# Sums of squares before the norms of a hybrid encoder layer: one f32 matmul each, or two matmuls on rounded squares and rests, and column sums in another PSUM bank

## The chip, the core and the metric

The kernel runs on one core of one Trainium2 chip. The metric is the device time of one execution in microseconds (us), the median of several runs. All times of the profile come from one profiled execution.

## The reference, cut to what matters

One encoder layer on x of 512 tokens by 2048 features, in float32:

```python
h = rms_norm(x, norm_mix_pre) * (1 + sc1) + sh1
proj = h @ w_in                       # q (8 heads), k, v (2 heads each), five groups of 8 recurrent heads
q = rms_norm(q, q_norm_w); k = rms_norm(k, k_norm_w)      # over the 128 features of a head
q = rope(q) * 128 ** -0.5; k = rope(k)
o_att = softmax(q @ k.T) @ v
o_hg = bidirectional_gated_recurrence(...)                # 8 heads, chunkwise in the reference
o_hg = rms_norm(o_hg, out_norm) * silu(gate)              # over the 128 features of a head
x = x + g1 * rms_norm(concat(o_att, o_hg) @ w_out, norm_mix_post)
x = x + g2 * rms_norm(conv_glu_ffn(rms_norm(x, norm_ffn_pre) * (1 + sc2) + sh2), norm_ffn_post)
```

What matters here are the sums over 128 features that the norms of 2 keys, 8 queries and 8 recurrent heads need: 18 in all, each for 512 tokens.

## The kernel before

**Layout.** Activations lie with features on the 128 partitions and the 512 tokens along the row, so that a head is one 128x512 tile. A sum over a head's features is then a sum over partitions. It is made on TensorE: the squares (`SQA` for keys and queries, `SQ` for recurrent heads) stream through a 128x128 matrix of ones, and every partition of a PSUM bank (`PB[2]`, `PB[5]`) gets the sum. A matmul with plain f32 operands is recorded as two weight loads and two matmuls.

**Three passes.** The projections multiply in three passes of rounded numbers (type fp32r): ScalarE writes the rounded copy (`W_hi`, `H_hi`), VectorE the rest (`W_lo`, `H_lo`), and `three_passes` (L2131) adds lo*hi, hi*hi and hi*lo in a bank. Such a matmul is one weight load and one matmul.

**Steps.** From about 147 us to 900 us the work is an order written out by hand. TensorE's outer loop are projection tiles of 16 steps; `project_step` is one step, three passes of 128x512. Between the steps, at step numbers fixed in the code, every engine has its side work: `kv_side` (2 keys and 2 values, beside the first tile), `att_side` (h, s) and `att_tail` (eight attention heads, one tile of 16 steps each), then `hg_side` (p, g) with g from 0 to 79 for a recurrent head p beside the five tiles of the next one. VectorE and ScalarE have the same loops with their own branches for the same step numbers. Each engine works through its list strictly in the order of the code; semaphores join them. The splits of the weights (`split_hi` on ScalarE, `split_lo` on VectorE) stand in the same lists, at steps 4 and 6 (VectorE one step later) of a tile, in recurrent heads at every eighth step.

**A norm of keys or queries** (index r: 0 and 1 are keys, 2 to 9 queries). ScalarE squares the head into `SQA` (`rope_front`, L825), TensorE sums it (`rope_mm`, L2158, at steps 1 and 7 for the keys, step 1 for a query), ScalarE makes Ln and Exp of the sum (`rope_rs`, L845 and L847, with a table load before each), which is the factor `RSA`. VectorE (`rope_back`) meanwhile multiplies the head by cosines and its rotated copy by sines (L1463, L1465), adds (L1467), and multiplies by `RSA` (L1472). Then the query is split into `Q_hi` and `Q_lo` (L887, L1502), and the `scores` matmuls start at step 7. `att_values` (L2198), at step 4, writes the bank that `rope_mm` wrote, and so waits until the Ln of the same tile's query has read it.

**A norm of recurrent heads.** At g = 72 ScalarE squares bank 4 into `SQ` (L1018), at g = 73 TensorE sums it (`sum_squares`, L2346) into bank 5, at g = 74 ScalarE makes Ln and Exp (L1023, L1025), at g = 76 VectorE writes the result (L1624).

**Column sums of the modulation.** Beside each of the eight projection heads VectorE adds up 16 rows of `w_ada` in `AB_acc`; at g = 77 and 78 `sum_chunk` (L2375) sums its columns with two groups of four 128x1 matmuls, also into bank 5, and `chunk_take` (L1643) copies the eight numbers out. Because the bank is shared, `sum_chunk` waits for `o_rstd`, which the Exp of the norm raises, and `turn_hg_values` of the next head (four transposes into bank 5) waits for `chunk_taken`.

Of the kernel before, what the change touches and what calls it, by code (L numbers as in the profile page):

```python
# [154 lines left out]
def hybrid_encoder_layer(nc, x, c, w_ada, b_ada, norm_mix_pre, norm_mix_post, w_in, q_norm, k_norm,  # L155
# [17 lines left out]
    ones = at("ones", [P, P], F32, C0 + 512)  # L173
    VEC = at("VEC", [P, 768], F32, C0 + 1536)
# [44 lines left out]
    SQA = at("SQA", [P, S], F32, OV + 12 * KB)  # L219
    RSA = at("RSA", [P, S], F32, OV + 14 * KB)  # L220
# [17 lines left out]
    SQ = at("SQ", [P, S], F32, OV + 24 * KB)  # L238
    RS = at("RS", [P, S], F32, OV + 26 * KB)
# [59 lines left out]
    with ExitStack() as ctx:  # L299
# [22 lines left out]

        rope_in, rope_psum, rope_rstd, rope_ln, rope_t, rope_done = (
# [427 lines left out]
        def _(act):  # L751
# [35 lines left out]
            act.activation(SM[:, LBT:LBT + 32], SM[:, LBT:LBT + 32], ACT.Exp).then_inc(lb_exp, 1)  # L787
            act.wait_ge(shift_added, KT)
# [33 lines left out]
            def rope_front(r, src):  # L822
                if r:
                    act.wait_ge(rope_psum, r)
                act.activation(SQA[:, :], src, ACT.Square).then_inc(rope_in, 1)  # L825
# [47 lines left out]
            def att_store(h):  # L873
                act.wait_ge(att_pv, h + 1)
                act.activation(MX[:, HEADS[h], :], PB[2][:, :], ACT.Copy).then_inc(att_out, 1)
# [13 lines left out]
            def att_side(h, s):  # L889
                if s == 0:  # L890
                    query_front(h)
                if s == 2:
                    rope_rs(h + KV_HEADS)
# [23 lines left out]
            def key_front(g):  # L917
                act.wait_ge(k_kept, g + 1)
                rope_front(g, KR[:, g, :])
# [65 lines left out]
            def hg_side(p, g):  # L985
# [30 lines left out]
                if g == 72:  # L1016
                    act.wait_ge(av_done, p + 1)
                    act.activation(SQ[:, :], PB[4][:, :], ACT.Square).then_inc(o_squared, 1)  # L1018
# [302 lines left out]
        def _(dve):  # L1321
# [136 lines left out]
            def rope_back(r, src, turned, w, w_turned, dst, gates=()):  # L1458
                if r == 0:
                    dve.wait_ge(tables_landed, 32)  # L1460
                else:
                    dve.wait_ge(rope_done, r)
                dve.scalar_tensor_tensor(T1[:, :], src, w, COS[:, :], ALU.mult, ALU.mult).then_inc(rope_t, 1)  # L1463
# [136 lines left out]
            def hg_side(p, g):  # L1600
# [16 lines left out]
                if g == 73:  # L1617
                    dve.wait_ge(o_squared, p + 1)
                    dve.tensor_tensor(OG[:, :], PB[4][:, :], GW[:, :], ALU.mult).then_inc(o_gated, 1)
# [20 lines left out]
            def chunk_take(h):  # L1640
                dve.wait_ge(chunk_summed, h + 1)
                dst = MOD[:, 32 + 8 * h:40 + 8 * h] if isinstance(h, int) else MOD[:, bass.ds(h * 8 + 32, 8)]
                dve.tensor_copy(dst, PB[5][:, 0:8]).then_inc(chunk_taken, 1)  # L1643
# [410 lines left out]
        def _(pe):  # L2054
# [95 lines left out]
            def rope_mm(r):  # L2150
                pe.wait_ge(rope_in, r + 1)
                if r == 0:
                    pe.wait_ge(front_kept, 1)
# [4 lines left out]
                pe.matmul(PB[2][:, :], ones[:, :], SQA[:, :], start=True, stop=True).then_inc(rope_psum, 1)  # L2158
# [501 lines left out]
```

## Time and profile before

| | before |
|---|---|
| median of 3 runs | 2378.36 us (2376.03 to 2379.28) |
| span of the profiled execution | 2375.8 us |
| PE, matmul | 2334.7 us busy (98%) |
| PEld, weight loads | 2025.8 us (85%) |
| DVE (VectorE) | 1878.8 us (79%) |
| ACT (ScalarE) | 1104.8 us (47%) |
| POOL | 128.6 us (5%) |

The span goes from the first to the last recorded instruction of the profiled execution. The page gives no device time of that execution apart from its span; the span lies 2.6 us below the median of the timed runs and 0.2 us below the fastest of them.

How to read it: the busy time of PE is modelled from pipelined matmuls and overstates how full it is; a 128x512 matmul is recorded with 0.39 us, though the next one starts sooner. The start times of successive weight loads (PEld) show TensorE's pace. In a timeline row "x2" means two instructions in one row, and the bracket at the end is the idle time of the engine just before, with what ended it. An instruction's record on ACT or DVE can overlap the next one's by up to 0.1 us. PEclk is the granted TensorE clock as a share of 2.4 GHz.

### The profile page before, as it was taken

How to read it: one execution, taken by the hardware profiler on the slowest of the kernel's cores; microseconds unless marked ns; L12 is line 12 of the kernel's file. 1: busy time of each engine (PE TensorE's matmuls, PEld its weight loads, DVE VectorE, ACT ScalarE, POOL GpSimd, SP SyncE). 2: the span in 40 equal slices, each digit the busy share in tenths (PEclk: the TensorE clock that was granted, in tenths of full speed). 3: DMA queues.
4: the chain of work that ended last, by engine and by line, in shares of the span. 5: the costliest groups of instructions: out<-in, count | busy, mean ns of one | idle time of the engine just before them, and what ended most of it. 6: DMA issues, size and time to landing. Idle time of an engine off the chain costs nothing.

```text
span 2375.8 us, 37218 instructions
## 1 busy us (share of the span) xinstructions
PE 2334.7 (98%) x13671; PEld 2025.8 (85%) x13671; DVE 1878.8 (79%) x2447; ACT 1104.8 (47%) x1517; POOL 128.6 (5%) x207
## 2 busy tenths in 40 slices
PE   6999999999999999999999999999999999999998
PEld 3577778888888877878999999999999998888887
DVE  5875667887777873267799999999999998888777
ACT  4266744334443353254444444444444445555554
POOL 1010000000000000000000000000000000001100
PEclk9999999999999999999999999999999999999999
DMA  9952456666666734336555555555555559779966
GB/s 366 346 157 85 133 180 208 215 219 212 207 211 198 234 89 169 98 124 159 146 140 146 145 144 143 144 142 139 141 145 145 142 176 329 251 207 285 279 226 224
DMA packets 378834, 442.47 MB, mean 186 GB/s; under 512 B 14876, under 2 KB 295716, under 8 KB 376448
## 3 DMA queue, kind: packets, MB, share of 16 engines
q1 hardware_dynamic: 359056, 369.74, 49.1%
q0 software_dynamic: 19696, 71.68, 13.0%
q8 instruction: 46, 0.75, 0.1%
q14 instruction: 36, 0.29, 0.0%
HBM read 418.81 MB, written 66.08 MB: 204 GB/s over the span
## 4 chain that ended last, share of the span: by engine, by line
PE 87%; DVE 5%; DMA 3%; ACT 2%; issue 2%; SPq 0%; DVEq 0%; ACTq 0%
PE bank L2132 26%; PE bank L2134 26%; PE bank L2133 26%; DMA ADA<-in_w_ada_dram 2%; PE bank L2295 2%; DVE ACC L1373 2%; DMA AB_raw<-in_w_ada_dram 1%; PE bank L2198 1%; DVE ZZ L1577 1%; PE bank L2375 1%; PE bank L2314 1%; PE bank L2189 1%; DVE W_lo L1332 0%; PE bank L2063 0%; DVE AB_acc L1636 0%
## 5 line engine op out<-in xcount | busy, mean ns | idle before, releaser
L2132 PE MATMUL bank<-H_lo,W_hi 128*128 128x256 f32 (+1 forms) x1832 | 635.7, 347 | 0.0
L2134 PE MATMUL bank<-H_hi,W_lo 128*128 128x256 f32 (+1 forms) x1832 | 613.6, 335 | 0.0
L2133 PE MATMUL bank<-H_hi,W_hi 128*128 128x256 f32 (+1 forms) x1832 | 613.2, 335 | 0.0
L2132 PEld LDWEIGHTS bank<-H_lo,W_hi 128*128 128x128 f32 x1832 | 349.3, 191 | 35.8 <-issue 6.2
L2133 PEld LDWEIGHTS bank<-H_hi,W_hi 128*128 128x128 f32 x1832 | 349.3, 191 | 35.7 <-issue 6.2
L2134 PEld LDWEIGHTS bank<-H_hi,W_lo 128*128 128x128 f32 x1832 | 348.8, 190 | 35.6
L2132 PE MATMUL bank<-T_lo,W_hi 128*128 128x256 f32 x1280 | 362.2, 283 | 0.0
L2133 PE MATMUL bank<-MGR,W_hi 128*128 128x256 f32 x1280 | 362.2, 283 | 0.0
L2134 PE MATMUL bank<-MGR,W_lo 128*128 128x256 f32 x1280 | 362.2, 283 | 0.0
L2132 PEld LDWEIGHTS bank<-T_lo,W_hi 128*128 128x128 f32 x1280 | 245.8, 192 | 0.0
L2133 PEld LDWEIGHTS bank<-MGR,W_hi 128*128 128x128 f32 x1280 | 245.8, 192 | 0.0
L2134 PEld LDWEIGHTS bank<-MGR,W_lo 128*128 128x128 f32 x1280 | 245.8, 192 | 0.0
L1332 DVE TENSOR_TENSOR W_lo<-W_raw,W_hi 128x1024 fp32r<-128x1024 f32 x138 | 168.1, 1220 | 94.6 <-ACT W_hi L765 94.2
L2132 PE MATMUL bank<-W_lo,GS_hi 128*128 128x512 f32 x616 | 240.0, 390 | 1.7 <-DVE W_lo L1941 1.7
L2134 PE MATMUL bank<-W_hi,GS_lo 128*128 128x512 f32 x616 | 239.7, 389 | 0.0
L2133 PE MATMUL bank<-W_hi,GS_hi 128*128 128x512 f32 x616 | 239.7, 389 | 0.0
L1168 ACT ACTIVATE W_hi<-UB 128x1024 fp32r<-128x1024 f32 x160 | 164.1, 1049 | 148.6 <-DVE UB L1810 95.1
L1798 DVE TENSOR_TENSOR W_lo<-UB,W_hi 128x1024 fp32r<-128x1024 f32 x160 | 195.1, 1220 | 26.9 <-ACT W_hi L1168 26.9
L765 ACT ACTIVATE W_hi<-W_raw 128x1024 fp32r<-128x1024 f32 x138 | 144.8, 1050 | 77.4 <-PE bank L2134 44.6
L1636 DVE SCALAR_TENSOR_TENSOR AB_acc<-AB_raw,SM,AB_acc 128x1024 f32<-128x1024 f32 x120 | 153.6, 1280 | 16.9 <-DMA AB_raw<-in_w_ada_dram 15.7
L1168 ACT ACTIVATE W_hi<-W_raw 128x1024 fp32r<-128x1024 f32 x80 | 84.5, 1056 | 150.6 <-DVE W_raw L1810 98.3
L2132 PEld LDWEIGHTS bank<-W_lo,GS_hi 128*128 128x128 f32 x616 | 115.6, 188 | 27.0 <-DVE W_lo L1941 2.5
(311 smaller groups left out, 3741.7 us busy)
## 6 DMA issues: line engine op xcount, KB each, us to landing
AB_raw<-in_w_ada_dram SPq DMA_DIRECT2D x128, 512.0 KB, 4.4
UB<-in_w_up_dram SPq DMA_DIRECT2D x100, 512.0 KB, 4.1
W_raw<-in_w_in_dram SPq DMA_DIRECT2D x90, 512.0 KB, 4.8
t_dram<-in_w_down_dram POOLq DMA_DIRECT2D x88, 512.0 KB, 8.1
DRAW<-in_w_down_dram SPq DMA_DIRECT2D x66, 512.0 KB, 5.8
W_raw<-in_w_up_dram SPq DMA_DIRECT2D x56, 512.0 KB, 3.9
ADA<-in_w_ada_dram SPq DMA_DIRECT2D x48, 512.0 KB, 9.0
W_raw<-in_w_down_dram SPq DMA_DIRECT2D x44, 512.0 KB, 6.1
```

The lines of the kernel that those rows point to most:

```text
L765: act.activation(W_hi[:, k % SLOTS, :], W_raw[:, k % RAW, :], ACT.Copy).then_inc(hi_ready, 1)
L1168: act.activation(units(W_hi[:, (U_ST + PRODUCTS * jj + p) % SLOTS, :]), ST[e][ST_UNIT[p]], ACT.Copy)\
L1332: dve.tensor_tensor(W_lo[:, k % SLOTS, :], W_raw[:, k % RAW, :], W_hi[:, k % SLOTS, :].bitcast(F32), ALU.subtract).then_inc(lo_ready, 1)
L1373: ins = dve.scalar_tensor_tensor(ACC[g][:, :], src, col(SM, CS + r), ACC[g][:, :], ALU.mult, ALU.add)
L1577: ins = dve.tensor_tensor(v, v, t[:, :, :, other].unsqueeze(3).broadcast_to([P, 2, n, m]), ALU.mult)
L1636: ins = dve.scalar_tensor_tensor(AB_acc[:, :], AB_raw[:, kt % 2, :], col(SM, CS + kt), AB_acc[:, :], ALU.mult, ALU.add)
L1798: dve.tensor_tensor(units(W_lo[:, slot, :]), ST[e][ST_UNIT[p]], units(W_hi[:, slot, :].bitcast(F32)), ALU.subtract)\
L2132: pe.matmul(acc, st_hi, mv_lo, start=start, stop=False, skip_group_check=on)
L2133: pe.matmul(acc, st_hi, mv_hi, start=False, stop=False, skip_group_check=on)
L2134: return pe.matmul(acc, st_lo, mv_hi, start=False, stop=stop, skip_group_check=on)
L2189: ins = pe.transpose(PB[6 + qt % 2][:, k * P:(k + 1) * P], PM[qt][:, k * P:(k + 1) * P], ident[:, :])
L2295: ins = pe.matmul(bank[:, a * P:(a + 1) * P], KM[:, a * P:(a + 1) * P], queries, start=True, stop=True)
```

## The change

The squares get a rounded copy (`SQA_hi`, `SQ_hi`) and a rest (`SQA_lo`, `SQ_lo`), and the sum is two fp32r matmuls with a rounded matrix of ones, `ones_r`. This goes for 17 of the 18 sums: the last recurrent head keeps its f32 matmul at g = 73. ScalarE squares twice (the second time in f32), VectorE has a new subtraction, and `rope_mm` waits for it (`squares_low`) before its second matmul. `rope_mm` moves from steps 1 and 7 to 2 and 8 for the keys, and from 1 to 2 for queries; `sum_squares` from g = 73 to 75. `SQA_hi` lies in a row of `MX` that holds the input activations before and an attention output after, so two waits are added. The column sums go to bank 6 and no longer wait for `o_rstd`.

```diff
+    ones_r = at("ones_r", [P, P], F32R, C0 + 1024)
+    SQA_lo = at("SQA_lo", [P, S], F32R, OV + 12 * KB)
+    SQA_hi = at("SQA_hi", [P, S], F32R, MXB + HEADS[-2] * 2 * KB)
+    SQ_lo = at("SQ_lo", [P, S], F32R, OV + 24 * KB)
+    SQ_hi = at("SQ_hi", [P, S], F32R, OV + 36 * KB)
...
+            act.wait_ge(consts_landed, 16)
+            act.activation(ones_r[:, :], ones[:, :], ACT.Copy).then_inc(lb_exp, 1)
...
             def rope_front(r, src):
                 if r:
                     act.wait_ge(rope_psum, r)
+                act.activation(SQA_hi[:, :], src, ACT.Square)
                 act.activation(SQA[:, :], src, ACT.Square).then_inc(rope_in, 1)
...
             def att_store(h):
                 act.wait_ge(att_pv, h + 1)
+                if h == ATT_HEADS - 2:
+                    act.wait_ge(rope_psum, ATT_HEADS + KV_HEADS)
...
-                if s == 2:
+                if s == 3:
                     rope_rs(h + KV_HEADS)
...
             def key_front(g):
                 act.wait_ge(k_kept, g + 1)
+                act.wait_ge(h_lo, KT)
...
                 if g == 72:
                     act.wait_ge(av_done, p + 1)
+                    if not (isinstance(p, int) and p == HG_HEADS - 1):
+                        act.activation(SQ_hi[:, :], PB[4][:, :], ACT.Square)
...
                     dve.wait_ge(rope_done, r)
+                dve.wait_ge(rope_in, r + 1)
+                dve.tensor_tensor(SQA_lo[:, :], SQA[:, :], SQA_hi[:, :].bitcast(F32), ALU.subtract).then_inc(squares_low, 1)
                 dve.scalar_tensor_tensor(T1[:, :], src, w, COS[:, :], ALU.mult, ALU.mult).then_inc(rope_t, 1)
...
                 if g == 73:
                     dve.wait_ge(o_squared, p + 1)
+                    if not (isinstance(p, int) and p == HG_HEADS - 1):
+                        dve.tensor_tensor(SQ_lo[:, :], SQ[:, :], SQ_hi[:, :].bitcast(F32), ALU.subtract).then_inc(squares_low, 1)
...
-                dve.tensor_copy(dst, PB[5][:, 0:8]).then_inc(chunk_taken, 1)
+                dve.tensor_copy(dst, PB[6][:, 0:8]).then_inc(chunk_taken, 1)
...
-                pe.matmul(PB[2][:, :], ones[:, :], SQA[:, :], start=True, stop=True).then_inc(rope_psum, 1)
+                pe.wait_ge(rope_in, r + 1)
+                pe.matmul(PB[2][:, :], ones_r[:, :], SQA_hi[:, :], start=True, stop=False)
+                pe.wait_ge(squares_low, r + 1)
+                pe.matmul(PB[2][:, :], ones_r[:, :], SQA_lo[:, :], start=False, stop=True).then_inc(rope_psum, 1)
...
-                if s == 1:
+                if s == 2:
                     rope_mm(h + KV_HEADS)
...
-                if s in (1, 7):
-                    rope_mm(s // 7)
+                if s in (2, 8):
+                    rope_mm(s // 8)
...
                 pe.wait_ge(vt_ready, p + 1)
-                pe.wait_ge(chunk_taken, p + 1)
+                if not (isinstance(p, int) and p == 0):
+                    pe.wait_ge(o_ln, p)
...
-                if g == 73:
+                if g == (73 if isinstance(p, int) and p == HG_HEADS - 1 else 75):
                     sum_squares(p)
...
-                    if not first:
-                        pe.wait_ge(o_rstd, h)
+                    if first:
+                        pe.wait_ge(pt_ready, ATT_HEADS * TT)
+                    else:
+                        pe.wait_ge(chunk_taken, h)
                 for j in range(4 * half, 4 * half + 4):
-                    ins = pe.matmul(PB[5][:, j:j + 1], AB_acc[:, j * P:(j + 1) * P], ones[:, 0:1], start=True, stop=True)
+                    ins = pe.matmul(PB[6][:, j:j + 1], AB_acc[:, j * P:(j + 1) * P], ones[:, 0:1], start=True, stop=True)
```

`sum_squares` has the same pair of matmuls with `SQ_hi` and `SQ_lo` for all heads but the last.

How VectorE's list moves at the keys, in the order of issue. `T` is the rotated sum, `KTT` the finished key, `W_lo` the rest of a weight tile. Before:

```order
L1463 SCALAR_TENSOR_TENSOR T_108<-KR,VEC,COS 128x512 [waits tables_landed,k_kept]
L1465 SCALAR_TENSOR_TENSOR KTT<-KROT,VEC,SIN 128x512 [waits rot_landed0]
L1467 TENSOR_TENSOR T_108<-T_108,KTT 128x512 [waits rope_t]
L1472 TENSOR_TENSOR KTT<-T_108,RSA 128x512 [waits rope_rstd,rope_t]
L1332 TENSOR_TENSOR W_lo<-W_raw,W_hi 128x1024 [waits hi_ready] x2
L1463 SCALAR_TENSOR_TENSOR T_108<-KR,VEC,COS 128x512 [waits rope_done,k_kept]
```

And with the change:

```order
L1478 TENSOR_TENSOR SQA_lo<-SQA,SQA_hi 128x512 [waits rope_in,tables_landed,k_kept]
L1479 SCALAR_TENSOR_TENSOR T_111<-KR,VEC,COS 128x512
L1481 SCALAR_TENSOR_TENSOR KTT<-KROT,VEC,SIN 128x512 [waits rot_landed0]
L1483 TENSOR_TENSOR T_111<-T_111,KTT 128x512 [waits rope_t]
L1488 TENSOR_TENSOR KTT<-T_111,RSA 128x512 [waits rope_rstd,rope_t]
L1346 TENSOR_TENSOR W_lo<-W_raw,W_hi 128x1024 [waits hi_ready] x2
L1478 TENSOR_TENSOR SQA_lo<-SQA,SQA_hi 128x512 [waits rope_in,rope_done,k_kept]
L1479 SCALAR_TENSOR_TENSOR T_111<-KR,VEC,COS 128x512
```

The new subtraction of each key stands at the head of `rope_back`; the second key's stands behind two subtractions for weights.

TensorE's list at the end of a recurrent head, from the sum of squares on. Before, with four steps between the sum of squares and the column sums, of which the first stands here:

```order
L2346 MATMUL bank<-SQ,ones 128x512 [waits o_squared]
L2132 MATMUL bank<-H_lo,W_hi 128x512
L2133 MATMUL bank<-H_hi,W_hi 128x512
L2134 MATMUL bank<-H_hi,W_lo 128x512
...
L2375 MATMUL bank<-ones,AB_acc 128x1 [waits o_rstd,chunk_added]
L2375 MATMUL bank<-ones,AB_acc 128x1 x3
```

And with the change:

```order
L2371 MATMUL bank<-SQ_hi,ones_r 128x512 [waits o_squared]
L2373 MATMUL bank<-SQ_lo,ones_r 128x512 [waits squares_low]
L2150 MATMUL bank<-H_lo,W_hi 128x512
L2151 MATMUL bank<-H_hi,W_hi 128x512
L2152 MATMUL bank<-H_hi,W_lo 128x512
...
L2404 MATMUL bank<-ones,AB_acc 128x1 [waits chunk_taken,chunk_added]
L2404 MATMUL bank<-ones,AB_acc 128x1 x3
```

Two steps now lie between the pair and the column sums, and the column sums wait for the copy of the head before in place of this norm's Exp.

## Rows read from the trace of the kernel before

**Rows 1.** The page: busy time of PE; the chain that ended last, by engine
```profile
PE 2334.7 (98%) x13671; PEld 2025.8 (85%) x13671; DVE 1878.8 (79%) x2447; ACT 1104.8 (47%) x1517; POOL 128.6 (5%) x207
PE 87%; DVE 5%; DMA 3%; ACT 2%; issue 2%; SPq 0%; DVEq 0%; ACTq 0%
```
**Rows 2.** Busy time by stretch: stretch, length, PE, PEld, DVE, ACT, POOL, granted clock, DMA
```profile
145.00:310.00 165.00, 162.19 (x699) 119.72 (x698) 107.10 (x170) 120.02 (x189) 19.08 (x39) 1.00 0.41 118
```
**Rows 3.** Timeline, weight loads around the sum of squares of one recurrent head
```profile
473.93 0.19 PEld L2134 LDWEIGHTS bank<-H_hi,W_lo 128*128 128x128 f32 x1
474.16 0.41 PEld L2346 LDWEIGHTS bank<-SQ,ones 128*128 128x128 f32 x2
474.81 0.19 PEld L2132 LDWEIGHTS bank<-H_lo,W_hi 128*128 128x128 f32 x1 [0.24 <-issue]
...
475.71 0.19 PEld L2132 LDWEIGHTS bank<-H_lo,W_hi 128*128 128x128 f32 x1
```
**Rows 4.** The end of that head: the wait for column sums, their timeline
```profile
PEld bank L2375 <- issue: 3.1, 7, 0.4
...
477.44 0.63 ACT L1025 ACTIVATE RS<-RS 128x512 f32<-128x512 f32 x1
478.19 0.97 PEld L2375 LDWEIGHTS bank<-ones,AB_acc 128*128 128x128 f32 x8 [0.44 <-issue]
481.01 0.17 DVE L1643 COPY MOD<-bank 128x8 f32 x1 [0.73 <-PE bank L2375]
481.75 1.28 ACT L964 ACT_TABLE_LOAD   x1 [2.73 <-PE bank L2134]
```
**Rows 5.** Prices of a square and of a 128x512 subtraction or product (min/median/max, ns)
```profile
L825 ACT ACTIVATE SQA<-MX x8: 614/622/622, 161.5 to 299.5; 128x512 f32<-128x512 f32 x8
L1472 DVE TENSOR_TENSOR QT<-T,RSA x8: 691/692/694, 166.7 to 306.6; 128x512 f32<-128x512 f32 x8
```
**Rows 6.** Timeline, the keys: four transposes, the second key's sum, Ln, and DVE
```profile
151.43 0.59 PEld L2167 LDWEIGHTS bank<-ident,VT 128*128 128x128 f32 x4
...
153.95 0.42 PEld L2158 LDWEIGHTS bank<-SQA,ones 128*128 128x128 f32 x2
157.10 0.69 ACT L845 ACTIVATE RSA<-bank,SM 128x512 f32<-128x512 f32 x1
155.82 1.23 DVE L1332 TENSOR_TENSOR W_lo<-W_raw,W_hi 128x1024 fp32r<-128x1024 f32 x1 [0.68 <-ACT W_hi L765]
156.96 0.75 DVE L1463 SCALAR_TENSOR_TENSOR T<-KR,VEC,COS 128x512 f32<-128x512 f32 x1
```
**Rows 7.** Timeline, the first query: Ln, and the first scores
```profile
163.93 0.69 ACT L845 ACTIVATE RSA<-bank,SM 128x512 f32<-128x512 f32 x1
...
169.49 0.19 PEld L2132 LDWEIGHTS bank<-K_lo,Q_hi 128*128 128x128 f32 x1 [2.41 <-issue]
```
**Rows 8.** Timeline, a query tile without a sigmoid: square, Ln, values
```profile
198.91 0.62 ACT L825 ACTIVATE SQA<-MX 128x512 f32<-128x512 f32 x1
201.83 0.69 ACT L845 ACTIVATE RSA<-bank,SM 128x512 f32<-128x512 f32 x1
203.45 0.42 PEld L2198 LDWEIGHTS bank<-PT,VSA 128*128 128x128 f32 x2
```
**Rows 9.** Timeline, a query tile with a sigmoid: Ln, values
```profile
262.88 0.69 ACT L845 ACTIVATE RSA<-bank,SM 128x512 f32<-128x512 f32 x1
263.62 0.30 PEld L2198 LDWEIGHTS bank<-PT,VSA 128*128 128x128 f32 x2 [0.69 <-ACT RSA L845]
```
**Rows 10.** Busy time by stretch with and without a fall of the clock (columns as in rows 2)
```profile
130.90:134.40 3.50, 2.17 (x15) 1.63 (x14) 3.14 (x5) 0.00 (x0) 0.00 (x0) 1.00 0.56 163
134.40:137.80 3.40, 3.40 (x10) 2.53 (x9) 1.26 (x3) 3.17 (x5) 0.00 (x0) 0.51 0.53 154
...
165.10:168.50 3.40, 2.40 (x11) 1.66 (x9) 1.65 (x2) 3.39 (x5) 0.59 (x2) 1.00 0.00 0
```
**Rows 11.** Timeline, TensorE's idle inside the first stretch of rows 10
```profile
133.14 0.97 PEld L2116 LDWEIGHTS bank<-ones,ACC 128*128 128x128 f32 x8 [1.75 <-DVE ACC L1373]
```

More of the change, by code:

```diff
@@ L321, in hybrid_encoder_layer @@
         h_scaled, h_hi, h_lo = sem("h_scaled"), sem("h_hi"), sem("h_lo")
+        squares_low = sem("squares_low")
         rope_in, rope_psum, rope_rstd, rope_ln, rope_t, rope_done = (
@@ L2150, in rope_mm @@
             def rope_mm(r):
-                pe.wait_ge(rope_in, r + 1)
                 if r == 0:
+                    pe.wait_ge(lb_exp, 2)
                     pe.wait_ge(front_kept, 1)
@@ L2345, in sum_squares @@
                 pe.wait_ge(o_squared, p + 1)
-                pe.matmul(PB[5][:, :], ones[:, :], SQ[:, :], start=True, stop=True).then_inc(o_summed, 1)
+                if isinstance(p, int) and p == HG_HEADS - 1:
+                    pe.matmul(PB[5][:, :], ones[:, :], SQ[:, :], start=True, stop=True).then_inc(o_summed, 1)
+                else:
+                    pe.matmul(PB[5][:, :], ones_r[:, :], SQ_hi[:, :], start=True, stop=False)
+                    pe.wait_ge(squares_low, p + (ATT_HEADS + KV_HEADS + 1))
+                    pe.matmul(PB[5][:, :], ones_r[:, :], SQ_lo[:, :], start=False, stop=True).then_inc(o_summed, 1)
             def hg_side(p, g):
@@ L2371, in sum_chunk @@
                     pe.wait_ge(chunk_added, h * KT + KT)
-                    if not first:
-                        pe.wait_ge(o_rstd, h)
+                    if first:
+                        pe.wait_ge(pt_ready, ATT_HEADS * TT)
+                    else:
+                        pe.wait_ge(chunk_taken, h)
                 for j in range(4 * half, 4 * half + 4):
-                    ins = pe.matmul(PB[5][:, j:j + 1], AB_acc[:, j * P:(j + 1) * P], ones[:, 0:1], start=True, stop=True)
+                    ins = pe.matmul(PB[6][:, j:j + 1], AB_acc[:, j * P:(j + 1) * P], ones[:, 0:1], start=True, stop=True)
                 if half == 1:
@@ L2420, in out_step @@
                         pe.wait_ge(vt_ready, HG_HEADS)
+                    if cb == 0 and tt == 2:
+                        pe.wait_ge(chunk_taken, HG_HEADS)
                     if cb == 0 and tt == 1:
```

## Prediction, on record before the changed kernel ran

> **What bounds the kernel now.** I read the page first: TensorE (PE) is recorded busy for 98% of the span, and 87% of the chain that ended last is PE [rows 1]. So a microsecond less in TensorE's list is a microsecond less in the span, unless TensorE then arrives at a wait. Next the busy times by stretch: beside the attention heads (145 to 310 us) ScalarE is busy 120 of 165 us, VectorE 107 [rows 2]. Last the timelines of the places where the edited instructions stand, to see for each who waits for whom.
>
> **What a sum costs.** In the pace of the weight loads one fp32r matmul follows the last after 0.23 us (473.93 to 474.16). From the load of the f32 sum to the load of the second step after it pass 1.55 us (474.16 to 475.71) [rows 3]; a step of three such matmuls in it takes 0.69, so the f32 sum takes 0.86 us. The pair that replaces it takes 2 x 0.227 = 0.45. Each of the 17 sums gets **0.41 us** cheaper on TensorE, 7.0 us in all. The Trainium skill ("FP8 and Floating Point Precision", "TensorE Precision Notes") says that true FP32 takes four passes through the array; an estimate from that page with the pitch of a rounded matmul would be 4 x 0.227 = 0.91 us and 7.7 us saved, where the row says 7.0; I keep the row. What the new wait between the two matmuls costs when the rest is long there, no row shows: nothing at the low end, at the high end the 0.24 us of the nearest gap in TensorE's issue [rows 3], 17 times 4.1 us. I take nothing, since that gap stands behind the second load of an f32 matmul, and keep the 4.1 for the range.
>
> **Recurrent heads, 7 times.** The sum moves two steps (1.38 us) later and is 0.41 us shorter, so the Ln starts 1.0 us later. Behind it on ScalarE stand the Exp and one weight copy, and then it sat idle 2.73 us before the next head's sigmoid; VectorE sat idle for 0.73 us before it copied the column sums [rows 4]. The second square (0.62 us [rows 5]) hides under the steps before the pair: bank 4 is complete at step 72, square, square and rest take 0.6 + 0.6 + 0.7 = 1.9 us, and the pair comes after step 75, four steps or 2.7 us on. So nothing is late; if the cover were gone, each head would pay 1.0 us. The column sums waited for the Exp: it ended at 478.07, the load of the column sums started at 478.19 after 0.44 us idle, and that happened 7 times, 3.1 us [rows 4]. In bank 6 they wait for a copy made a head ago, so these 3.1 us go. The transposes' new wait, for the Ln before, is one that was long met. Gain: 7 x (0.41 + 0.44) = **5.95 us**.
>
> **The second key.** The pair needs the rest, and VectorE makes it at the head of its list for that key. That place was reached at 156.96, after a weight subtraction that itself waited for its rounded copy from ScalarE; TensorE was at the key's sum at 153.95 [rows 6]. With the change TensorE comes there at 153.95 - 0.41 (first key's sum) + 0.69 (one step later) = 154.2 and at the second matmul at 154.45. ScalarE, which works here without a gap, is 0.3 us late from the first key's Ln (a step later, 0.41 cheaper) and 0.62 us from the second square [rows 5], and so is the weight copy; VectorE begins the rest at 156.96 + 0.9 = 157.9 and ends at 158.55. TensorE stands for **4.1 us**. The Ln of that key moves from 157.10 to 159.2. Now two lists run to the first query's Ln, before at 163.93 [rows 7]: ScalarE's gets there 2.1 + 0.62 later, 166.65; TensorE's has, from 158.8 on, ten steps and four transposes (10 x 0.69 + 0.59 [rows 6]), then the pair and the end of its last matmul (0.45 + 0.39), 167.1. The later one counts: 3.1 us late. What follows, up to the first scores at 169.49, where TensorE stood for 2.41 us before [rows 7], is a chain of ScalarE and VectorE, so the scores start at 172.6. The three cheap sums before it are lost in these waits. Loss: **3.1 us**.
>
> **Queries without a sigmoid in their tile, 4 times.** The values matmul must wait for the Ln. Before, the Ln ended at 202.52 and the values' load began at 203.45 [rows 8]. Now TensorE would be there at 203.04, but the second square puts the Ln's end at 203.14 (square, square, the two copies and the table load stand in one row on ScalarE). The rest itself is in time: squares end at 200.15, the rest at 200.85, the pair comes at about 201.2. So 0.26 us of 0.41 stay: **1.0 us** gained.
>
> **Queries with a sigmoid, 3 times.** Here ScalarE is already last: TensorE stood 0.69 us for the Ln, whose end at 263.57 released the load at 263.62 [rows 9]. The second square is added to it in full and the cheaper sum only lengthens the wait: 3 x 0.62 = **1.9 us** lost. In both kinds the loaded weights and the query's own split move with the Ln and are not late for step 7.
>
> **The clock.** TensorE was granted 1.00 until 134.4 us and 0.51 from there to 137.8, after it had been busy 2.17 of 3.5 us, part of that with eight 128x1 matmuls behind an idle of 1.75 us [rows 11]; it kept 1.00 when it was busy 2.40 of 3.40 us at 165 to 168.5 with full ones [rows 10]. That is 1.2 in place of 2.4 GHz for 3.4 us, or **1.7 us** lost where TensorE is what is waited for. The new stand of 4.1 us is longer than that idle, so I count one such fall, in the stretch before the first query's Ln where TensorE's list decides. The Trainium skill ("TensorE: Matmul & The Clock Gate", Part 1) says the same way round that activity releases the throttle and an idle engine is put back to half rate; by that rule too a fall is due here.
>
> **Nothing else.** The copy of `ones` (0.2 to 0.3 us of ScalarE at 45 us) lies in a stretch that waits for the loads of `w_ada`; the keys' wait for `h_lo` is met before; the wait of `att_store` for the last pair comes three steps after that pair.
>
> **The sum.** -5.95 - 1.0 + 1.9 + 3.1 + 1.7 = **-0.3 us** against the span of 2375.8 us. The median of the runs shown is 2378.36 us, 2.6 above the span; I take the same difference and predict 2378.1 us. About 0.2%, 4.8 us, is what a measurement of this kernel can tell from no change.
>
> **The rivals.**
> *The stand without a fall of the clock:* the sum is -2.0 us, 2376.4. For it: the idle of 2.41 us at 169.5 cost no clock. Against it: the new one is longer. 20 in 100.
> *The waits are hidden:* TensorE finds every rest ready and every Ln done. Then all 10.0 us (7.0 + 3.1) come out, 2368.3. For it: PE is 98% busy and the chain is PE's. Against it: the orders of issue, with the second key's rest behind two weight subtractions, and the 0.69 us at 263.6, where ScalarE is last already. 15 in 100.
> *Slower, by the clock at the queries with a sigmoid:* TensorE's idle before the values there grows from 0.69 to 0.69 + 0.41 + 0.62 = 1.7 us, as long as the idle of 1.75 us [rows 11] that went ahead of the fall. If the clock falls each time, 3 x 1.7 = 5.1 us are added: +4.8, 2383.2. It decides from an idle of about 1.7 us on; for it is the like length, against it that dense f32 matmuls follow at once, where 128x1 ones followed there. [...] 10 in 100.
> *The pair is not cheaper* (a wait between its matmuls at 0.24): +3.8 us against the span, 2382.1. 5 in 100.
>
> **How the numbers follow.** The forecast itself has 50 in 100; its own range is 2375.5 to 2380.5, from 0.5 us of error in each of the five terms. The range over all takes in the wait's upper end and the falls above (+5) and reaches half way to the hidden case (-6.4) below: 2372 to 2383.5. Faster by over 0.2%: the hidden case and a little of the first rival, 0.18. Slower by over 0.2%: half of the last two and an unseen stall, 0.12. Within: 0.70.
>
> **What would show it.** Right: an idle of TensorE of about 4 us inside the second key's pair, released by VectorE, with the granted clock at 0.5 just behind; first scores near 172.6; no idle before the column sums; TensorE idle 1.7 us for the Ln in the last three query tiles and about 0.1 in the four before; recurrent heads 0.85 us shorter each. Wrong: no idle at that pair (then the order on VectorE does not matter as I think), new idle before the diagonal or the gate of a recurrent head (then the later Ln was not covered), or a pair that takes more than 0.5 us.

## The result

The changed kernel takes **2393.56 us** (median of 5 runs, 2390.71 to 2394.89) against 2378.36 (5 runs, 2376.03 to 2379.28): 15.2 us more, ratio 1.006 with a 95% interval of 1.005 to 1.0071. Forecast were 2378.1 us and a range of 2372 to 2383.5. It is slower, outside the range, and by a mechanism that none of the rivals named.

The page of the changed kernel (span 2392.8 us), the same two parts as in [rows 1]:

```profile
PE 2331.5 (97%) x13671; PEld 2026.3 (85%) x13671; DVE 1889.1 (79%) x2464; ACT 1114.0 (47%) x1535; POOL 129.0 (5%) x207
...
PE 77%; DVE 9%; DMA 8%; ACT 3%; issue 2%; SPq 1%; DVEq 0%; ACTq 0%
```

TensorE is busy for 3 us less than before, but its share of the chain fell from 87 to 77%, and DMA's rose from 3 to 8%: the last to arrive is now often a transfer. The busy time by stretch says where; first the changed kernel, columns as in [rows 2]:

```profile
145.00:310.00 165.00, 155.72 (x687) 118.41 (x686) 111.15 (x175) 122.39 (x196) 19.69 (x40) 0.99 0.40 112
...
416.00:848.00 432.00, 420.70 (x2092) 352.68 (x2091) 338.45 (x444) 163.31 (x218) 7.67 (x15) 1.00 0.67 210
```

The same stretch of recurrent heads in the kernel before:

```profile
416.00:848.00 432.00, 428.37 (x2125) 358.22 (x2125) 341.70 (x449) 166.74 (x221) 8.15 (x16) 1.00 0.67 208
```

In equal time TensorE gets through 33 matmuls fewer. The starts of each head's first recurrent matmul (L2282 before, L2304 after, from the timeline) give the same in time: before 343.0 for the first and 848.1 for the eighth, after 347.5 and 860.7. So the changed kernel was 4.5 us behind by then, and the seven heads took 513.2 us in place of 505.1: **8.1 us more, where 5.95 less were forecast**. The remaining 4.4 us of the difference of spans arise behind 1959 us. 2.8 of them are waits of TensorE for weight rests that the change doesn't touch (4.5 us in this execution, 1.7 in the kernel before, 1.6 to 1.9 in the twelve kernels below). This is taken for variation between executions, and the rest is not explained.

**What came as forecast.** Timeline of the weight loads at the end of one head, changed kernel (the head of [rows 3, 4]):

```profile
479.03 0.19 PEld L2371 LDWEIGHTS bank<-SQ_hi,ones_r 128*128 128x128 f32 x1
479.26 0.19 PEld L2373 LDWEIGHTS bank<-SQ_lo,ones_r 128*128 128x128 f32 x1
479.48 0.19 PEld L2150 LDWEIGHTS bank<-H_lo,W_hi 128*128 128x128 f32 x1
...
480.84 1.08 PEld L2404 LDWEIGHTS bank<-ones,AB_acc 128*128 128x128 f32 x8
```

The pair takes 0.45 us (479.03 to 479.48), no wait stands in it, and none before the column sums. The second key, the first query's Ln and the first scores of the changed kernel, three pieces of timelines:

```profile
154.72 0.19 PEld L2177 LDWEIGHTS bank<-SQA_hi,ones_r 128*128 128x128 f32 x1
159.02 0.19 PEld L2179 LDWEIGHTS bank<-SQA_lo,ones_r 128*128 128x128 f32 x1 [4.11 <-DVE SQA_lo L1478]
...
167.31 0.69 ACT L854 ACTIVATE RSA<-bank,SM 128x512 f32<-128x512 f32 x1 [0.40 <-PE bank L2179]
...
172.87 0.19 PEld L2150 LDWEIGHTS bank<-K_lo,Q_hi 128*128 128x128 f32 x1 [2.62 <-issue]
```

TensorE stands 4.11 us (forecast 4.1), the Ln starts at 167.31 (167.1), the scores at 172.87 (172.6).

**What did not.** The waits of TensorE by releaser (us in total, times, longest), changed kernel. Rows of PEld are waits before a weight load, rows of PE before the matmul that follows it; the two rows of L2317 show the same stands twice and are not added up:

```profile
PEld bank L2317 <- DVE AT L1609: 18.8, 18, 1.7
...
PEld bank L2219 <- ACT RSA L854: 4.6, 3, 1.5
PEld bank L2179 <- DVE SQA_lo L1478: 4.1, 1, 4.1
...
PE bank L2317 <- ACT KM L994: 11.0, 16, 1.3
```

and the rows of the kernel before that answer to the first and the last:

```profile
PEld bank L2295 <- DVE AT L1593: 5.1, 9, 1.4
...
PE bank L2295 <- ACT KM L982: 1.9, 3, 1.0
```

The level matmuls (L2317, before L2295) wait for VectorE's and ScalarE's steps of the same level, 18 times for 9 before. At the weight loads this is 13.7 us more, which is nearly the whole distance from -5.95 to +8.1. Why these are late stands in VectorE's timeline behind the head's end, changed kernel:

```profile
483.52 1.23 DVE L1346 TENSOR_TENSOR W_lo<-W_raw,W_hi 128x1024 fp32r<-128x1024 f32 x1
...
486.57 0.75 DVE L1550 SCALAR_TENSOR_TENSOR GW<-bank,VEC,SG 128x512 f32<-128x512 f32 x1 [1.75 <-ACT SG L976]
...
494.97 0.75 DVE L1651 TENSOR_SCALAR AB_acc<-AB_raw,SM 128x1024 f32<-128x1024 f32 x1 [3.80 <-DMA AB_raw<-in_w_ada_dram]
```

VectorE reached the first row of the modulation sum at 491.17 and stood 3.80 us for its load; the picks and scalings of the levels are queued behind. In the kernel before it came there at 488.32 and did not wait. From the gate product (`GW`) to the first scaling of the levels VectorE takes 8.80 us before and 11.62 with the change. The queues at this place, SP's and POOL's timelines, changed kernel:

```profile
484.91 0.37 SPq L546 DMA_DIRECT2D W_raw<-in_w_in_dram  x1
485.58 0.87 SPq L555 DMA_DIRECT2D AB_raw<-in_w_ada_dram  x2
...
484.72 1.53 POOL L716 DMA_DIRECT2D t_dram<-in_w_down_dram  x3 [71.27 <-PE bank L2152]
```

and in the kernel before:

```profile
480.44 0.37 SPq L540 DMA_DIRECT2D W_raw<-in_w_in_dram  x1
481.11 0.88 SPq L549 DMA_DIRECT2D AB_raw<-in_w_ada_dram  x2
...
481.94 1.53 POOL L710 DMA_DIRECT2D t_dram<-in_w_down_dram  x3 [71.40 <-PE bank L2134]
```

Two things moved. The loads are issued when `W_lo` is ready, which stands behind the weight copy, the Exp and the sum of squares, all later now; the gate product, which marks the next head, comes earlier against them: 486.57 - 484.91 = 1.7 us after the load of `W_raw` instead of 483.80 - 480.44 = 3.4. And GpSimd's three 512 KB copies, released by TensorE at the head's end, now go out 0.2 us ahead of the loads, not 1.5 behind. The median times to landing (DMA issues, 484.7 to 495 us of the changed kernel, where the second `W_raw` is the next one, issued at 491.34):

```profile
W_raw<-in_w_in_dram SPq DMA_DIRECT2D x2, 512.0 KB, 7.1
AB_raw<-in_w_ada_dram SPq DMA_DIRECT2D x2, 512.0 KB, 9.9
```

and, 480.4 to 488.4 us of the kernel before:

```profile
AB_raw<-in_w_ada_dram SPq DMA_DIRECT2D x2, 512.0 KB, 5.1
W_raw<-in_w_in_dram SPq DMA_DIRECT2D x1, 512.0 KB, 3.8
```

The chain of waits of the changed kernel for 484 to 500 us names the whole path, VectorE's rest, the issue, the transfer, the sum's row:

```profile
483.52 1.24 DVE W_lo L1346
...
485.58 9.37 DMA AB_raw<-in_w_ada_dram
...
494.97 0.77 DVE AB_acc L1651
```

### The profile page after: what moved, and what is told of

The parts are those of the page before. It is cut to its first block, busy times and chain, and to the rows that moved or that the text cites. A ratio compares the mean times of both kernels' runs of the same rounds, so it can differ in the third digit from the quotient of the medians.

```text
span 2392.8 us, 37261 instructions
## 1 busy us (share of the span) xinstructions
PE 2331.5 (97%) x13671; PEld 2026.3 (85%) x13671; DVE 1889.1 (79%) x2464; ACT 1114.0 (47%) x1535; POOL 129.0 (5%) x207
## 4 chain that ended last, share of the span: by engine, by line
PE 77%; DVE 9%; DMA 8%; ACT 3%; issue 2%; SPq 1%; DVEq 0%; ACTq 0%
PE bank L2150 23%; PE bank L2151 23%; PE bank L2152 23%; DMA AB_raw<-in_w_ada_dram 4%; DMA ADA<-in_w_ada_dram 2%; DMA W_raw<-in_w_down_dram 2%; PE bank L2317 1%; DVE ACC L1387 1%; PE bank L2219 1%; DVE ZZ L1593 1%; DVE W_lo L1959 1%; DVE W_lo L1346 1%; DVE AB_acc L1654 1%; DMA DRAW<-in_w_down_dram 1%; PE bank L2336 1%
## 5 line engine op out<-in xcount | busy, mean ns | idle before, releaser
L2150 PE MATMUL bank<-H_lo,W_hi 128*128 128x256 f32 (+1 forms) x1832 | 628.1, 343 | 1.0 <-DVE H_lo L1413 1.0
```

Source lines behind the costliest of these rows:

```text
L2150: pe.matmul(acc, st_hi, mv_lo, start=start, stop=False, skip_group_check=on)
```

## The experiments

Twelve kernels, in three groups on three chips, each timed beside the kernel before; that took 2377.41 us with the first four, 2378.09 with the second, 2379.38 with the third. Times of different groups are therefore compared by their difference to the kernel before beside them; for the changed kernel this is +15.2 us. The interval of such a difference reaches about 2 us to either side with 11 runs and 3 with 5. A diff is against the changed kernel unless another is named. A and B in the expectations are rival explanations, and each text says anew what they stand for.

### First four: the copies, and the second key

**copies_late.** GpSimd's copies wait for the stages of the next head instead of for the head's last unit:

```
-    pool.wait_ge(unit_used, U_HG + 10 * (m // 3 + 1))
+    pool.wait_ge(stage_ready, 4 * (m // 3 + 1))
```

> The changed kernel, with GpSimd's three copies per recurrent head into t_dram held until the gate of that head is made (stage_ready in place of unit_used), so that they are issued behind SyncE's weight load and two w_ada loads again, as in the kernel before. Theory A (order of the transfers: the loads now stand behind the copies and land late): the waits of the level matmuls for AT (18.8 us, 18 times in the changed kernel) fall back to about 5 us, the six recurrent heads come 0.85 us shorter than before, and the time is about 14 us below the changed kernel, near 2379 us. Rival B (the second square on ScalarE and the subtraction on VectorE, 1.3 us a head, make the level chain late): nothing changes, 2393 us.

Measured: 2380.77 us (11 runs), ratio to before 1.0008 (0.9999 to 1.0017). That is +3.4 us, 11.8 less than the change. Its VectorE timeline at the place in question:

```profile
492.03 0.75 DVE L1651 TENSOR_SCALAR AB_acc<-AB_raw,SM 128x1024 f32<-128x1024 f32 x1
```

The load was issued at 486.52, so it landed within 5.5 us, and no wait is left. The copies are needed for the loss. Whether their place in the order is enough for it, this run doesn't say.

**before_copies_early.** The kernel *before*, its copies released one unit (eight steps) earlier, so that they are ahead of the loads:

```
-    pool.wait_ge(unit_used, U_HG + 10 * (m // 3 + 1))
+    pool.wait_ge(unit_used, U_HG + 10 * (m // 3 + 1) - 1)
```

> The kernel before with nothing of the change; only GpSimd's three copies per recurrent head are released one weight unit (8 steps, 5.5 us) earlier, ahead of SyncE's loads at the end of the head. Theory A: the level matmuls wait as in the changed kernel, 6 to 12 us above the kernel before (2384 to 2390 us), with the copies issued ahead of W_raw and AB_raw in the trace. Rival B: no difference, 2378.4 us.

Measured: 2378.36 us (11 runs), ratio 1.0002 (0.9993 to 1.0011): a miss. But the copies went out at 473.16, 7.7 us ahead of the loads and so nearly landed by then. The run doesn't reach the case in question.

**key_rest_early.** The second key's rest of squares put at step 5 on VectorE, ahead of the two weight rests:

```
-                dve.wait_ge(rope_in, r + 1)
-                dve.tensor_tensor(SQA_lo[:, :], SQA[:, :], SQA_hi[:, :].bitcast(F32), ALU.subtract).then_inc(squares_low, 1)
+                if r != 1:
+                    squares_rest(r)
...
+                    if k == 0 and s == 5:
+                        squares_rest(1)
```

> The changed kernel, with VectorE's subtraction for the second key put ahead of the two weight subtractions that it stood behind. Expected: TensorE's idle of 4.1 us inside the second key's pair goes, the first scores start about 3 us earlier, and the fall of the clock at 174 us goes with it, so 3 to 5 us below the changed kernel, 2388.5 to 2390.5 us. If instead another list decides the first query (ScalarE's), under 1 us is gained.

Measured: 2390.77 us (5 runs), ratio 1.0052 (1.0038 to 1.0066). TensorE's wait in that pair fell from 4.11 to 2.17 us. The time is +13.4 us, 1.8 less than the change, which is below what was expected; its interval overlaps that of the change. The trace says the same more sharply: from the four transposes ahead of the pair to the first scores pass 20.0 us, and 21.4 in the changed kernel.

**both_moved.** Both edits together.

> Both edits. If they are independent, as theory A and the stand at the second key say, the gains add up: 17 to 19 us below the changed kernel, 2374.5 to 2376.5 us, 2 to 4 us below the kernel before. Rival B: 2388.5 to 2390.5 us.

Measured: 2377.03 us (11 runs), ratio 1.0 (0.9991 to 1.0009). That is -0.4 us, 15.6 less than the change, where the two edits gained 11.8 and 1.8 alone. Beside copies_late on the same chip it is 3.7 us less. So the two gains add up within the error.

### Second four: is it the order of issue?

**copies_with_loads.** The kernel *before*, with the copies waiting for what the load of `W_raw` waits for:

```
-    pool.wait_ge(unit_used, U_HG + 10 * (m // 3 + 1))
+    pool.wait_ge(lo_ready, U_HG + 10 * (m // 3 + 1) + 2)
```

> The kernel before, with no part of the change; GpSimd's three 512 KB copies at each recurrent head's end wait for what the sync engine's load of W_raw waits for (the second weight rest of the head), so that they are issued at about 480.4 us, with W_raw (480.44) and ahead of AB_raw (481.11), and no longer at 481.94. A, the place of the copies against the two loads is what costs: W_raw and AB_raw land 2 to 4 us later, VectorE waits for AB_raw near 490 and the level matmuls for what stands behind it, 1 to 2 us in each of 7 heads: 2386 to 2392 us. B, the loss in the changed kernel comes from loads that are issued 4.5 us later (behind the later Exp), whatever the copies do: here the loads are on time, 2377.5 to 2379 us.

Measured: 2378.55 us (11 runs), ratio 1.0003 (0.9993 to 1.0012). SP, POOL and VectorE in its timeline:

```profile
479.57 0.37 SPq L540 DMA_DIRECT2D W_raw<-in_w_in_dram  x1
480.24 0.88 SPq L549 DMA_DIRECT2D AB_raw<-in_w_ada_dram  x2
...
479.70 1.53 POOL L710 DMA_DIRECT2D t_dram<-in_w_down_dram  x3 [70.58 <-DVE W_lo L1332]
...
488.60 0.75 DVE L1633 TENSOR_SCALAR AB_acc<-AB_raw,SM 128x1024 f32<-128x1024 f32 x1 [1.07 <-DMA AB_raw<-in_w_ada_dram]
```

The load is nearly as slow as in the changed kernel, 8.4 us from issue to use, and VectorE waits 1.07 us for it. The levels' first scaling comes 9.47 us behind the gate product, 0.67 later than before, and the level matmuls wait no longer (3.7 us in all against 5.1). A as it stood, that the place of the copies alone costs 8 to 14 us, is wrong. The time is B's, but B's reason, that the copies don't matter, had been refuted by copies_late.

**copies_just_ahead.** The same with `hi_ready`, so that the copies are issued 1.1 us ahead of `W_raw`.

> As the run above, but the copies wait for the weight's rounded copy, ready about 1.3 us before the rest: issue at about 479.1 to 480.2 us, all three ahead of W_raw (480.44). A: the loads stand behind all three copies, the loss is as large as in the run above or larger, 2387 to 2394 us. The copies 8 us ahead of the loads cost nothing (a run above); if 1.3 us ahead costs nothing either, the copies hurt only from between the loads. B: 2377.5 to 2379 us.

Measured: 2380.06 us (11 runs), ratio 1.0007 (0.9998 to 1.0016). VectorE waits 1.34 us there. The loss is 2.0 us by the medians and under 4 by the interval, not 9 to 16.

**bank_only.** Of the change only the column sums in bank 6 and the waits that go with them.

> Of the change only the column sums in bank 6, with the transposes' and the projection's waits that go with it; all sums stay f32 matmuls in their old places. The 0.44 us idle before the column sums goes in 7 heads, and nothing on ScalarE or VectorE is later, so the loads are still issued ahead of the copies (481.1 against 481.5): A, -3.1 us, 2374.0 to 2376.0 us. If the copies then come close enough behind AB_raw to hold it up: no gain or a loss, 2378 to 2384 us.

Measured: 2374.18 us (11 runs), ratio 0.9983 (0.9974 to 0.9992), 3.9 us less than before beside it; the 3.1 us of the forecast are there.

**heads_late.** The change without its attention part, with the copies moved as in copies_late.

> The change without its attention part (all ten sums for queries and keys stay f32 in their old places), with GpSimd's copies released after the stages of the next head, at about 488 us. If the recurrent heads gain what was forecast once the copies are out of the way, 7 x 0.85 = 5.95 us: 2371.5 to 2373.5 us, below both kernels. If they gain less (weights late by the second square or the later Ln): 2374 to 2378 us.

Measured: 2377.35 us (11 runs, 2373.05 to 2379.14), ratio 0.9997 (0.9988 to 1.0006). The first forecast is missed by 4 us, and the time lies in the range of the second, in which late weights take part of the gain. The profiled execution had a span of 2371.3 us and six heads of 70.3 to 71.4 us, but it was the fastest of the eleven (2373.05 us). With the copies out of the way the loads still come 1.7 us late against the next head; that this leaves some executions on the wrong side of VectorE's list is a guess, which no profile of a slower one shows.

### Third four: late loads *and* copies

The runs so far suggest a conjunction. Loads that are early enough stand slow transfers, and quick transfers stand late loads, or nearly so; the large loss takes both together. The next four could each break that.

**loads_early.** At each recurrent head's end ScalarE's weight copy stands between Ln and Exp instead of behind Exp, and VectorE's rest of it ahead of the output product:

```
-                        hg_side(h - 1, g)
+                        hg_side(h - 1, g, lambda: split_hi(i, 20, U_HG + 10 * e + LEAD + 9))
...
                     act.activation(RS[:, :], PB[5][:, :], ACT.Ln, bias=col(SM, EPSC), scale=1.0 / P).then_inc(o_ln, 1)
+                    between()
                     act.wait_ge(o_ln, p + 1)
                     act.activation(RS[:, :], RS[:, :], ACT.Exp, scale=-0.5).then_inc(o_rstd, 1)
...
+                        if g == 76:
+                            split_lo(i, 20, U_HG + 10 * e + LEAD + 9)
                         hg_side(h - 1, g)
```

(`between` is the function that the first line hands over; both steps are left out at their old places, 75 and 76.)

> The changed kernel with one reordering at each recurrent head's end: ScalarE's last rounded weight copy stands between Ln and Exp instead of behind Exp, VectorE's rest of it ahead of the output product. The two loads are issued about 2 us earlier (483.0 and 483.6 instead of 484.91 and 485.58), ahead of the copies at 484.7, and 3.6 us before the next head's gate product as in the kernel before (3.4). The runs so far say that neither loads 1.7 us later against the next head (copies_late) nor copies beside the loads (copies_with_loads) cost anything alone. A, it takes both: this kernel is as good as the one with the copies moved away, 2379 to 2383 us. B, the copies near the loads are enough in the changed kernel: 2388 to 2393 us.

Measured: **2376.05 us** (11 runs), ratio to before 0.9991 (0.9982 to 1.0). That is -3.3 us, 18.5 less than the change, with the copies still released by the head's last unit:

```profile
482.29 0.37 SPq L546 DMA_DIRECT2D W_raw<-in_w_in_dram  x1
482.95 0.87 SPq L555 DMA_DIRECT2D AB_raw<-in_w_ada_dram  x2
...
484.04 1.53 POOL L716 DMA_DIRECT2D t_dram<-in_w_down_dram  x3 [68.80 <-PE bank L2155]
...
490.41 0.75 DVE L1652 TENSOR_SCALAR AB_acc<-AB_raw,SM 128x1024 f32<-128x1024 f32 x1
```

The first six heads of this execution are 70.3 to 70.8 us long (in the changed kernel 70.3, then 72.7 to 73.2), and the wait for the load is gone. The copies' signal has not moved, but the loads now go out 1.8 us ahead of them, so this run takes both causes away. It is better than A expected, by 3 us. The second key's wait is still there (4.11 us), so the better part lies in the heads: it is 6.7 us below copies_late, each against the kernel before beside it, where A had counted late loads with fast transfers as free.

**late_f32.** bank_only with its f32 sum two steps later; no square is rounded anywhere:

```
-                if g == 73:
+                if g == 75 - 2 * (isinstance(p, int) and p == HG_HEADS - 1):
                     sum_squares(p)
```

> bank_only (2374.2 us) with the f32 sum of the recurrent heads at step 75 in place of 73: TensorE's work is the same, but Ln, Exp and with them the weight copy and the loads are 1.4 us later, about 0.2 us behind or ahead of GpSimd's first copy, and no nearer to the head's end than that. A (late loads beside the copies cost, whatever the squares are rounded to): the level matmuls wait, 2379 to 2388 us. B (the loss belongs to the rounded pair): 2374 to 2376 us.

Measured: **2393.23 us** (5 runs), ratio 1.0056 (1.0043 to 1.007). That is +13.9 us, 17.8 more than bank_only, and more than A expected. The row of the level matmuls and VectorE's of the load:

```profile
PEld bank L2305 <- DVE AT L1601: 20.6, 19, 1.7
...
494.79 0.75 DVE L1641 TENSOR_SCALAR AB_acc<-AB_raw,SM 128x1024 f32<-128x1024 f32 x1 [3.61 <-DMA AB_raw<-in_w_ada_dram]
```

TensorE has the same work as in bank_only, where that first row holds 2.8 us. The whole loss comes with the later place of the sum, and the rounded squares have no part in it.

**heads_only.** The change without its attention part.

> The change without its attention part, copies where they were. Pitch of heads as in the changed kernel (72.8 to 73.2 us) from the second on if the loss is made in each head by late loads beside the copies: 14 us above heads_late (2377.4) less what the fourth of a head's length moves, 2386 to 2391 us. If the loss needs the shift of 4.5 us from the attention stretch: 2372 to 2378 us.

Measured: 2389.31 us (5 runs), ratio 1.0047 (1.0033 to 1.0061), with heads of 72.6 to 73.8 us from the second to the sixth: the loss is made in the heads, whatever stood ahead of them.

**heads_early.** heads_only with the reordering of loads_early.

> heads_only with the reordering of loads_early: recurrent sums as rounded pairs, column sums in bank 6, attention sums f32 as before, loads about 2 us earlier, GpSimd's copies where they were. A: heads of 70.5 us, and the landings have more room than in bank_only and heads_late: 2371 to 2374 us, below both kernels and below bank_only. If the loads are not what is late: 2386 us or more.

Measured: **2373.62 us** (8 runs), ratio 0.9975 (0.9965 to 0.9986). It is below both kernels, by 5.8 us against before; from bank_only its interval doesn't part it.

**All of them in one table**, from one profiled execution each. From the timelines around 480 us: the place of the copies against `W_raw` (+ is behind it); the room, from the issue of `AB_raw` to VectorE's readiness for it; VectorE's wait; and the scaling, from the gate product to the first scaling of the levels. Then the level matmuls' waits for VectorE over the whole execution, and the median time less that of the kernel before beside it.

| kernel | copies, us | room, us | wait, us | scaling, us | level waits, us | less before, us |
|---|---|---|---|---|---|---|
| before | +1.5 | 7.2 | 0 | 8.80 | 5.1 | 0 |
| bank_only | +1.2 | 6.9 | 0 | 8.81 | 2.8 | -3.9 |
| before_copies_early | -7.7 | 7.2 | 0 | 8.81 | 1.8 | +1.0 |
| copies_with_loads | +0.1 | 7.3 | 1.07 | 9.47 | 3.7 | +0.5 |
| copies_just_ahead | -1.1 | 7.6 | 1.34 | 10.10 | 6.4 | +2.0 |
| copies_late | +2.7 | 5.5 | 0 | 8.81 | 4.3 | +3.4 |
| both_moved | +2.7 | 5.5 | 0 | 8.81 | 5.3 | -0.4 |
| heads_late | +2.7 | 5.5 | 0 | 8.80 | 3.1 | -0.7 |
| **changed kernel** | -0.2 | 5.6 | 3.80 | 11.62 | 18.8 | +15.2 |
| key_rest_early | -0.2 | 5.6 | 4.21 | 12.06 | 19.2 | +13.4 |
| late_f32 | -0.2 | 5.6 | 3.61 | 11.59 | 20.6 | +13.9 |
| heads_only | -0.2 | 5.6 | 3.61 | 10.97 | 19.5 | +9.9 |
| loads_early | +1.8 | 7.5 | 0 | 8.81 | 2.5 | -3.3 |
| heads_early | +1.8 | 7.5 | 0 | 8.80 | 1.6 | -5.8 |

Copies about level with the loads or 1 us ahead stretch the time from the issue of `AB_raw` to its use to between 8.4 and 9.8 us. With 7.3 to 7.6 us of room that is a wait of 1.1 to 1.3 us, most of which the levels absorb: in the kernel before, VectorE stands idle for 1.50 us before their first scaling anyway. With 5.6 us of room it is 3.6 to 4.2 us, and the second to the sixth head are about 2.5 us longer than in loads_early (73.0 against 70.5), the last one 4 us, with a fall of the clock at 853 us as a part of it.

## Why the prediction was wrong

**Recurrent heads, forecast -5.95 us, measured +8.1 in the trace and +9.9 alone (heads_only against before beside it).** This is the step that failed, and in it one sentence: "So nothing is late". It had been weighed for the pair (square, square and rest in 1.9 of 2.7 us: right), and for the Ln (ScalarE "sat idle 2.73 us" behind it: right, the idle is 1.03 us now and no sigmoid is late). It was not carried on to the weight copy and its rest. These were named as standing behind the Exp, but what waits for them is the SP queue, whose loads then slide 1.7 us against the next head, and GpSimd's copies, released by TensorE, which doesn't slide, go past them. The size of the slide was at hand: the Ln 1.0 us later and the head 0.85 us shorter are 1.85 us, measured are 1.7. The idle of 2.73 us on ScalarE hid the lateness of an instruction; it said nothing of the transfer that the instruction releases. The two prices of the term fit all the same: bank_only gains 3.9 us where the idle before the column sums was 3.1, and with the loads put back in time heads_early gains 5.8 where 5.95 were forecast. The second figure is no clean measurement, since the earlier loads also shorten the level waits below those of the kernel before (1.6 against 5.1 us); that reordering was not run on the kernel before. Of the signs named for "wrong", new idle before the diagonal or the gate came closest; the idle came a step further on, at the level matmuls.

**Second key, forecast +3.1.** Shown: the stand is 4.11 us. From the four transposes ahead of the pair to the first scores pass 18.06 us before and 21.36 with the change, 3.3 more. The nine kernels with f32 sums in the attention part, the kernel before among them, agree on the first figure within 0.02 us. Taking 1.94 us out of the stand (key_rest_early) shortens the way by 1.3 us.

**Queries, forecast -1.0 without and +1.9 with a sigmoid.** The three waits for the Ln hold 4.6 us against 2.1 before, the longest 1.5 instead of 0.7: 2.5 us more, of which the cheaper sum pays 3 x 0.41 back. That leaves 1.3. In the other four tiles no wait is left in the row. From the first scores to the first recurrent matmul the two kinds together took 173.54 us before and 172.98 in copies_late, where no fall of the clock lies between: 0.6 us less, where +0.9 was forecast. Of the rival that the clock falls there nothing is seen.

**The clock, forecast +1.7.** In the profiled execution of the changed kernel the fall came, but not behind the 4.1 us stand. The stretches around it, columns as in [rows 10]:

```profile
157.00:174.30 17.30, 13.05 (x58) 10.54 (x59) 12.46 (x16) 13.37 (x17) 4.23 (x9) 1.00 0.39 101
174.30:177.70 3.40, 3.40 (x9) 2.66 (x9) 1.51 (x4) 1.56 (x4) 0.00 (x0) 0.51 1.09 286
```

It follows the idle of 2.62 us before the scores, which was 2.41 in the kernel before [rows 7] and cost nothing. But the change isn't needed for this fall: bank_only, copies_just_ahead and late_f32, with f32 sums in the attention part and an idle of 2.42 to 2.43 us, have it too, the six other kernels with these sums don't. In both_moved, with the stand shortened, it is there as well (0.65 over 174.5 to 178.5 us).

The stand of 4.11 us occurs in two more profiled executions, and in both the clock fell toward its end, 1.5 and 0.8 us before TensorE went on. First copies_late, with the stand's end and the stretch, then the stretch in loads_early, where the stand ends at 159.63:

```profile
159.93 0.29 PEld L2179 LDWEIGHTS bank<-SQA_lo,ones_r 128*128 128x128 f32 x1 [4.11 <-DVE SQA_lo L1478]
158.40:165.20 6.80, 5.27 (x15) 4.25 (x16) 4.18 (x6) 4.54 (x6) 0.47 (x1) 0.51 0.60 164
158.80:165.60 6.80, 5.97 (x16) 4.84 (x17) 3.64 (x7) 4.55 (x7) 1.16 (x3) 0.50 0.63 174
```

It fell for twice as long there, and the scores came 2.4 and 2.8 us later against the transposes than in the changed kernel. None of the eleven kernels without that stand has a fall between 155 and 170 us. So the cause that I gave is borne out in two executions of three, and its price was sized too low there; for the changed kernel itself, that its one fall more is due to the change is not shown. The fall at 134.4 us [rows 10] is one at 99.2 in it, and apart from the last 20 us the fourteen profiled executions have between one and five falls, the kernel before four and the changed kernel five.

**The attention part as a whole**, forecast at +5.7 us (-1.0 + 1.9 + 3.1 + 1.7): three pairs of runs differ in it alone. Each taken against the kernel before beside it, the changed kernel less heads_only is 5.3, copies_late less heads_late 4.1, loads_early less heads_early 2.4. Each has an error of some 3 us. The sign is right and the size, if anything, too high by about 2 us.

**The rivals.** I gave 15 in 100 to hidden waits and 35 in 100 to others, all of them about waits between engines, the price of the pair and the clock. The range reached to about +5 us against the median before, and +15.2 came. A transfer that lands late was in none.

## What to carry to other kernels

When a step is moved, follow its neighbours in the list to the last thing that they release, the loads of the sync engine above all. Note for each load how long it has until its reader is ready (here 7.2 us), and what other queue issues near it and on whose signal: two queues released by different engines change places when one of these is sped up. An idle gap on the engine that issues or releases a load is not slack for the load; its slack is the room at the reader, less the landing in the worst order. Here 7.2 us of room against 5.1 of landing became 5.6 against 9.4, and the two together cost 15 us and more.

## What the runs showed of the hardware

The landing of a 512 KB load depended strongly on the order of issue across two queues. The median landing of the two `AB_raw` loads against the first of GpSimd's three 512 KB copies, each in one head of one execution: 5.1 us when issued 0.8 us ahead of it (the kernel before), 5.8 when 0.5 ahead (bank_only), 9.3 when 0.5 behind (copies_with_loads), 9.9 when 0.9 behind (the changed kernel), 9.2 when 1.8 behind (copies_just_ahead); with the copies 2 us behind the loads 5.0 to 5.1. So nearly all of the difference lies within one microsecond. The copies themselves landed in 7.4 us before and 7.8 with the change. The Trainium skill ("DMA: Bandwidth & Descriptors", "Queues, rings and completion order") says that each DMA engine takes turns between the queues it has work for, packet by packet. That agrees with loads that slow down beside copies; why a lead of half a microsecond saves most of it is in neither the page nor these runs.

Slow transfers with room at the reader cost 0.5 and 2.0 us (copies_with_loads and copies_just_ahead, both intervals across 1). Late loads with fast transfers are less clear. Against the kernel before, copies_late stands at 1.0008 and that looks free, but it contains the gains of the change. Its fair partner is loads_early, and that of heads_late is heads_early, and against these it is 6.7 and 5.0 us slower; the second pair's intervals don't meet. The profiled executions show little of it: no wait at the load, the scaling at 8.80 to 8.81 us as without late loads, 1.8 and 1.5 us more of level waits. What late loads cost alone stays open, between nearly nothing and 7 us. Both together cost 15.7 to 18.5 us (heads_only less heads_early, late_f32 less bank_only, the change less loads_early), more than the two alone add up to.

An experiment that undoes one of two joint causes shows most of the loss gone, and invites naming that one as the cause; only the two cells with one cause each tell it, each beside a partner that differs in that cause alone.

Not tried: loads_early with key_rest_early, the reordering of loads_early on the kernel before, and heads with the rounded pair at step 73 or 74.
